# The four sums of a Strassen quarter as four separate pieces, multiplied in the order T1, T2, T3, T4

## The chip, the core and the metric

The kernel runs on one core of a Trainium2 chip. TensorE multiplies matrices, VectorE and ScalarE work elementwise, GpSimd does a handful of tiny operations, and SyncE only issues DMAs. Each engine takes its own list of instructions strictly in order and waits on counting semaphores. The metric is the time of one execution on the device in microseconds (us); three executions of the kernel before took 1846.04, 1846.70 and 1846.81 us.

## The reference

Two layers over 256 tokens of width 2048, all in float32. The part that matters here is the MLP, which both layers have:

```python
def sqrelu_mlp(h, w_in, w_out):
    u = jax.nn.relu(h @ w_in)      # w_in  2048 x 8192
    return (u * u) @ w_out         # w_out 8192 x 2048

for l in range(DEPTH):             # DEPTH = 2
    if l < N_A_LAYERS:
        h = h + multiscale_pool_mixer(rms_norm(h, mix_norm[l]), pool_w[l], pool_scale[l])
    else:
        h = h + diff_attention(rms_norm(h, mix_norm[l]), k, v, w_q[j], lam[j], subln[j], w_o[j], cos, sin, l)
    h = h + sqrelu_mlp(rms_norm(h, mlp_norm[l]), w_mlp_in[l], w_mlp_out[l])
    if l == N_A_LAYERS - 1:
        k, v = shared_kv(h, kv_norm, w_kv, cos, sin)
return rms_norm(h, final_norm)
```

## The kernel before

**High and low halves.** Every weight is loaded as float32 into a raw buffer (`raw` or a part of `arena`; two halves of four pieces each, a piece being 128 x 1024 elements, 512 KB). ScalarE rounds it to `w_hi` (operations `hi_...`), VectorE computes `w_lo = raw - w_hi` (operations `lo_...`), and TensorE takes three matmuls for each product: hi x hi, hi x lo, lo x hi (`product`, L1356 to L1358). `w_hi` and `w_lo` have 8 slots, and a slot holds one piece.

**Pairs.** An MLP is cut into 8 column pairs p = 0 to 7 of 1024 hidden columns. For each p from 1 to 7, TensorE runs `in_pair(p)`, then `out_pair(p - 1)`, then `turn_u(p)`, 16 transposes of the finished hidden values. (In pairs 1 and 7 `turn_u` stands within other work.) Pairs 2 to 5 run in a hardware loop (`Fori`, two pairs in its body, so twice round), where the values waited for are computed in registers; pairs 1, 6 and 7 are written out. With two layers there are 14 such pairs: 8 in loops, 6 written out.

**One `in_pair`.** It has four units: mixed unit 1, a plain unit, mixed units 2 and 3. A mixed unit is one step of Strassen's scheme over a quarter of the weights with raw pieces a, b, c, d. VectorE makes four sums in place: T1 = a + b (in b), T2 = d + T1 (in d), T3 = T2 - a (in a), T4 = c + T2 (in c). TensorE takes seven products of six matmuls each: P1 and P2, P3 on plain pieces, P5 on T1 and P7, P4, P6 on the others. Each goes to a PSUM bank of its own. In unit 1 the banks must first be free of the previous pair's hidden values, so P7, P4 and P6 wait for `u_taken`, which VectorE's `u_low` raises.

**Order on the helpers at the end of unit 3.** VectorE (`mix_lo_lots`): split T1, sum T2, sum T3, sum T4, split T3, then one double-width split of T4 and T2 together (`lo_pair`). ScalarE (`mix_hi_lots`): round T1, round T3 once its sum is there, then round T4 and T2 with one double-width instruction (`hi_sums`). Next come the first steps of `out_pair`. ScalarE: `copy_p1` (L606, saves bank P1), then rounding of the first two double pieces of `w_mlp_out`. VectorE: split of the first double piece, then `c_11` (L951), the sum that empties bank P2. TensorE's first matmul of `out_pair` waits for both that split and `c_11` (`lo_ready`, `c_added`).

**Loads.** SyncE reloads a raw half as soon as `lo_ready` says that its pieces have been split; the counts are in `in_pair` and `out_pair` of the sync block (L403 to L431).

Of the kernel before, what the change touches and what calls it, by code (L numbers as in the profile page):

```python
# [23 lines left out]
F32 = mybir.dt.float32  # L24
F32R = mybir.dt.float32r
ACT = mybir.ActivationFunctionType
ALU = mybir.AluOpType
# [101 lines left out]
def trunk(nc, x, mix_norm, mlp_norm, pool_w, pool_scale, kv_norm, w_kv, w_q, lam, subln, w_o,  # L129
          w_mlp_in, w_mlp_out, final_norm, keep_consts, pool_consts, out):  # L130
    with ExitStack() as ctx:
# [101 lines left out]
        O_BANKS = ((B_P1, B_P2), (B_P3, B_P5))  # L233
        U_BANKS = (B_P7, B_P4, B_P6, B_22)
        END_BANKS = ((B_P1, B_P2), (B_P4, B_22), (B_P1, B_P2), (B_P4, B_22), (B_P3, B_P5), (B_P4, B_22), (B_P3, B_P5), (B_P4, B_22))
# [135 lines left out]
        def _(sp):  # L371
# [35 lines left out]
            def in_pair(layer, p):  # L407
                at = i_at(layer, p)
                if isinstance(p, int) and p == 0:
                    in_unit(layer, 0, 0, 0, at - 2, at)  # L410
                    if layer == 0:
                        sp.wait_ge(x_squared, 1)
                        sp.wait_ge(ssq_done, 3)
                    else:
                        sp.wait_ge(o_done, 2 * PAIRS)
                    in_unit(layer, 0, 1, 1, None, None)
                    in_unit(layer, 0, 2, 0, at + 2, at + 4)
                    in_unit(layer, 0, 3, 1, at + 6, at + 8)
                    return
                in_unit(layer, p, 1, 0, at - 6, at - 4)  # L420
                in_unit(layer, p, 0, 1, at - 2, at)
                in_unit(layer, p, 2, 0, at + 6, at + 8)
                in_unit(layer, p, 3, 1, at + 10, at + 12)

            def out_pair(layer, p):
                at = o_at(layer, p)
                for g in range(NG):
                    free = (at - 10, at - 2, at + 2, at + 6)[g]
                    load_unit(g % 2, [out_view[layer][:, bass.ds(p * 8 + 2 * i, 2), SW * g:SW * (g + 1)] for i in range(4)],
                              free, free + 2)  # L430

# [67 lines left out]
        def _(act):  # L499
# [19 lines left out]

            def hi_sums(at, slot, half, cd, summed):  # L520

                act.wait_ge(w_summed, summed)
                act.wait_ge(pe_done, at - 6)
                nc.scalar.activation(w_hi[:, slot:slot + 2], raw_half[half][:, 2 * cd:2 * cd + 2], ACT.Copy).then_inc(hi_ready, 2)  # L524

            def mix_hi_lots(at, slot, half, landed, sums, lots):

                for lot in lots:
# [7 lines left out]
                    elif lot == 2:  # L536
                        hi_sum(at + 4, spot, half, 1, sums + 1)
                        hi_sum(at + 5, spot + 1, half, 0, sums + 3)
                    else:
                        hi_sums(at + 6, spot, half, 1, sums + 4)  # L540

# [297 lines left out]
        def _(dve):  # L839
# [31 lines left out]

            def mix_lo_lots(at, slot, half, sums, lots):

                a, b, c, d = (raw_half[half][:, i] for i in range(4))
                for lot in lots:
                    spot = (slot + 2 * lot) % HALVES
                    if lot == 0:
                        dve.wait_ge(hi_ready, at + 2)
                        nc.vector.tensor_tensor(w_lo[:, spot], a, w_hi[:, spot].bitcast(F32), ALU.subtract).then_inc(lo_ready, 2)
                    elif lot == 2:  # L880
                        lo_sum(at + 4, spot, half, 1)
                        dve.wait_ge(w_summed, sums + 1)
                        dve.wait_ge(lo_ready, at + 4)
                        nc.vector.tensor_tensor(d, d, b, ALU.add).then_inc(w_summed, 1)  # L884
                        dve.wait_ge(w_summed, sums + 2)
                        nc.vector.tensor_tensor(a, d, a, ALU.subtract).then_inc(w_summed, 1)  # L886
                        nc.vector.tensor_tensor(c, c, d, ALU.add).then_inc(w_summed, 1)  # L887
                        lo_sum(at + 5, spot + 1, half, 0)
                    else:
                        lo_pair(at + 2 * lot, spot, half, lot % 2)  # L890

# [110 lines left out]
            def in_pair(layer, p, par):  # L1002
# [9 lines left out]
                if not second:  # L1012
                    out_add(layer, p - 2, 3)
                mix_lo_lots(at, slot, 0, sums, (3,))
                u_low(layer, p - 1, False)
                for cd in range(2):
                    lo_pair(at + 8 + 2 * cd, slot + 2 * cd, 1, cd)
                t1_sum(0, i_landed(layer, p, 2))
                mix_lo_lots(at + 12, (slot + 4) % HALVES, 0, sums + 4, (0, 1, 2))
                t1_sum(1, i_landed(layer, p, 3))  # L1020
                mix_lo_lots(at + 12, (slot + 4) % HALVES, 0, sums + 4, (3,))
                mix_lo_lots(at + 20, (slot + 4) % HALVES, 1, sums + 8, range(4))

# [292 lines left out]
        def _(pe):  # L1316
# [110 lines left out]
            def mix_unit(layer, p, u, at, slot, begin, end):  # L1427
# [22 lines left out]
                pe.wait_ge(lo_ready, at + 6)  # L1450
                mixed(B_P7, MIX_S3, u, (slot + 5) % HALVES, begin, end).then_inc(pe_done, 1)
                pe.wait_ge(lo_ready, at + 8)
                if begin:
                    pe.wait_ge(u_taken, done - 2)
                mixed(B_P4, MIX_22, u, (slot + 6) % HALVES, begin, end).then_inc(pe_done, 1)
                if begin:
                    pe.wait_ge(u_taken, done - 1)
                mixed(B_P6, MIX_S2, u, (slot + 7) % HALVES, begin, end).then_inc(pe_done, 1)

# [249 lines left out]
```

## Time and profile before

| | before |
|---|---|
| median of 3 runs | 1846.7 us |
| the profiled execution | 1846.67 us, of which 1844.9 us from its first to its last instruction (the span) |
| TensorE busy | 1799.5 us (98%) |
| VectorE busy | 1426.3 us (77%) |
| ScalarE busy | 977.3 us (53%) |
| DMA | 189 GB/s in the mean |
| mean granted TensorE clock | 0.999 |

The profile records one execution. A row of its timeline gives start, duration, engine, source line, operation, what is written and read, the count of merged instructions and, in brackets, how long the engine stood idle before and whom it waited for. ACT is ScalarE, DVE is VectorE, PE is TensorE. Back-to-back matmuls overlap: a 128 x 512 matmul lasts 0.39 us in the records and starts 0.23 us behind the one before.

### The profile page before, as it was taken

Reading aid. Unit: us, or ns where it says so; the run is one execution under the profiler, and the core shown is the slowest. Engines: PE = TensorE matmul, PEld = TensorE weight load, DVE = VectorE, ACT = ScalarE, POOL = GpSimd, SP = SyncE. Lnnn points to the kernel's source line nnn. Section 1 sums busy time; section 2 is a strip of 40 time slices with the busy share of each in tenths; the row PEclk is TensorE's granted clock in tenths of the full one; section 3 lists DMA queues with packets and bytes.
Section 4 is the critical chain, followed back from the end, with each engine's and each line's share of the span. In section 5 each row is a group of like instructions: output and inputs, shape, how many; then the busy total and the mean of one; then the engine's idle time right before and its main releaser. Section 6 shows DMA issues by size and latency. Waiting matters only on the chain.

```text
span 1844.9 us, 22951 instructions
## 1 busy us (share of the span) xinstructions
PE 1799.5 (98%) x8173; PEld 1487.5 (81%) x8173; DVE 1426.3 (77%) x1380; ACT 977.3 (53%) x1021; POOL 9.2 (0%) x15
## 2 busy tenths in 40 slices
PE   6999999999999999999999999999999999999998
PEld 5778787878787878888888888878787878788786
DVE  6787879788888886755557776788888879787876
ACT  6664655564646454643345545654646455554643
POOL 0000000000000000000000000000000000000000
PEclk9999999999999999999999999999999999999999
DMA  9446656565657474566664446365647474646671
GB/s 317 145 159 206 197 193 218 177 206 193 203 165 240 151 243 151 177 194 190 189 195 146 137 156 223 124 223 184 208 164 243 150 237 136 227 161 206 198 256 69
DMA packets 178487, 348.78 MB, mean 189 GB/s; under 512 B 10642, under 2 KB 10852, under 8 KB 178020
## 3 DMA queue, kind: packets, MB, share of 16 engines
q1 hardware_dynamic: 177696, 345.88, 56.7%
q10 hardware_dynamic: 708, 1.81, 0.3%
q8 instruction: 50, 0.82, 0.2%
q14 instruction: 33, 0.27, 0.0%
HBM read 345.55 MB, written 2.10 MB: 188 GB/s over the span
## 4 chain that ended last, share of the span: by engine, by line
PE 82%; DVE 9%; ACT 5%; issue 3%; DMA 1%; POOL 0%; DVEq 0%; SPq 0%; ACTq 0%; POOLq 0%
PE bank L1356 21%; PE bank L1358 20%; PE bank L1357 20%; PE bank L1332 6%; PE bank L1330 6%; PE bank L1331 6%; DVE w_lo L857 3%; ACT w_hi L512 2%; ACT w_hi L524 2%; PE bank L1377 1%; DVE arena L884 1%; PE bank L1348 1%; DVE w_lo L845 1%; DVE arena L886 1%; DVE arena L887 1%
## 5 line engine op out<-in xcount | busy, mean ns | idle before, releaser
L857 DVE TENSOR_TENSOR w_lo<-raw,w_hi 128x2048 fp32r<-128x2048 f32 x128 | 293.0, 2289 | 107.1 <-ACT w_hi L512 68.0
L1356 PE MATMUL bank<-w_hi,u_hi_a 128*128 128x512 f32 x896 | 350.3, 391 | 0.0
L1358 PE MATMUL bank<-w_hi,u_lo_a 128*128 128x512 f32 x896 | 348.8, 389 | 0.0
L1357 PE MATMUL bank<-w_lo,u_hi_a 128*128 128x512 f32 x896 | 348.7, 389 | 0.0
L857 DVE TENSOR_TENSOR w_lo<-arena,w_hi 128x2048 fp32r<-128x2048 f32 x128 | 291.6, 2287 | 54.6 <-ACT w_hi L512 42.5
L1356 PE MATMUL bank<-w_hi,mix_hi 128*128 128x512 f32 x684 | 269.4, 394 | 20.1 <-DVE w_lo L857 18.5
L512 ACT ACTIVATE w_hi<-arena 128x2048 fp32r<-128x2048 f32 x114 | 217.5, 1918 | 103.9 <-PE bank L1358 100.5
L512 ACT ACTIVATE w_hi<-raw 128x2048 fp32r<-128x2048 f32 x100 | 188.2, 1909 | 157.7 <-PE bank L1358 148.7
L1357 PE MATMUL bank<-w_lo,mix_hi 128*128 128x512 f32 x684 | 266.4, 389 | 0.0
L1358 PE MATMUL bank<-w_hi,mix_lo 128*128 128x512 f32 x684 | 266.3, 389 | 0.0
L505 ACT ACTIVATE w_hi<-raw 128x1024 fp32r<-128x1024 f32 x128 | 133.6, 1062 | 150.6 <-PE bank L1332 143.6
L845 DVE TENSOR_TENSOR w_lo<-raw,w_hi 128x1024 fp32r<-128x1024 f32 x128 | 153.2, 1221 | 73.3 <-ACT w_hi L505 72.8
L1356 PEld LDWEIGHTS bank<-w_hi,u_hi_a 128*128 128x128 f32 x896 | 168.1, 188 | 39.1 <-issue 2.8
L1358 PEld LDWEIGHTS bank<-w_hi,u_lo_a 128*128 128x128 f32 x896 | 168.2, 188 | 35.2
L1357 PEld LDWEIGHTS bank<-w_lo,u_hi_a 128*128 128x128 f32 x896 | 168.2, 188 | 34.3
L979 DVE TENSOR_TENSOR h<-bank,h 128x512 f32<-128x512 f32 x168 | 107.9, 684 | 93.0 <-PE bank L1358 75.0
L1356 PEld LDWEIGHTS bank<-w_hi,mix_hi 128*128 128x128 f32 x684 | 128.4, 188 | 52.0 <-DVE w_lo L857 24.4
L1358 PEld LDWEIGHTS bank<-w_hi,mix_lo 128*128 128x128 f32 x684 | 128.4, 188 | 27.0
L1357 PEld LDWEIGHTS bank<-w_lo,mix_hi 128*128 128x128 f32 x684 | 128.5, 188 | 25.7
L1332 PE MATMUL bank<-w_hi,a_lo 128*128 128x512 f32 x352 | 137.1, 390 | 0.0
L518 ACT ACTIVATE w_hi<-raw 128x1024 fp32r<-128x1024 f32 x56 | 59.6, 1064 | 141.8 <-DVE raw L886 120.4
L1330 PE MATMUL bank<-w_hi,a_hi 128*128 128x512 f32 x320 | 126.1, 394 | 0.0
(173 smaller groups left out, 2598.3 us busy)
## 6 DMA issues: line engine op xcount, KB each, us to landing
raw<-in_w_mlp_in SPq DMA_DIRECT2D x128, 512.0 KB, 4.5
arena<-in_w_mlp_in SPq DMA_DIRECT2D x128, 512.0 KB, 5.3
raw<-in_w_mlp_out SPq DMA_DIRECT2D x128, 512.0 KB, 5.0
arena<-in_w_mlp_out SPq DMA_DIRECT2D x128, 512.0 KB, 4.9
raw<-in_w_kv SPq DMA_DIRECT2D x64, 512.0 KB, 4.5
raw<-in_w_q SPq DMA_DIRECT2D x32, 512.0 KB, 4.6
raw<-in_w_o SPq DMA_DIRECT2D x32, 512.0 KB, 4.0
raw<-in_pool_w SPq DMA_DIRECT2D x8, 512.0 KB, 7.5
```

The source lines that it names most:

```text
L505: nc.scalar.activation(w_hi[:, strip_slot(s, n)], raw[:, n % RAW], ACT.Copy).then_inc(hi_ready, 1)
L512: nc.scalar.activation(w_hi[:, slot:slot + 2], raw_half[half][:, 2 * cd:2 * cd + 2], ACT.Copy).then_inc(hi_ready, 2)
L518: nc.scalar.activation(w_hi[:, slot], raw_half[half][:, i], ACT.Copy).then_inc(hi_ready, 1)
L845: nc.vector.tensor_tensor(w_lo[:, slot], raw[:, n % RAW], w_hi[:, slot].bitcast(F32), ALU.subtract).then_inc(lo_ready, 1)
L857: nc.vector.tensor_tensor(w_lo[:, slot:slot + 2], raw_half[half][:, 2 * cd:2 * cd + 2], w_hi[:, slot:slot + 2].bitcast(F32), ALU.subtract) ...
L979: last = nc.vector.tensor_tensor(h[:, tb, cols], banks[tb][:], h[:, tb, cols], ALU.add)
L1330: nc.tensor.matmul(banks[tb][:], hi[:, tok], w_hi[:, n, kk, :], start=begin, stop=False)
L1331: nc.tensor.matmul(banks[tb][:], hi[:, tok], w_lo[:, n, kk, :], start=False, stop=False)
L1332: last = nc.tensor.matmul(banks[tb][:], lo[:, tok], w_hi[:, n, kk, :], start=False, stop=end)
L1356: nc.tensor.matmul(bank[:], hi, w_hi[:, slot, kk, :], start=begin, stop=False)
L1357: nc.tensor.matmul(bank[:], hi, w_lo[:, slot, kk, :], start=False, stop=False)
L1358: return nc.tensor.matmul(bank[:], lo, w_hi[:, slot, kk, :], start=False, stop=end)
```

## The change

The pair {T4, T2} of `hi_sums`/`lo_pair` is taken apart. The four sums now go through the engines as T1, T2, T3, T4: each is rounded by an instruction of its own, split by one of its own, and waited for by itself. On VectorE the split of T2 comes between sum T3 and sum T4. TensorE's products follow: P5 on T1, then P6 on T2, P7 on T3 and P4 on T4. The banks that `turn_u` fills (`U_BANKS`) change their order in the same way. The raw pieces a and b are free when T3 is split and c and d when T4 is, so SyncE's waits move by one count.

```diff
-        U_BANKS = (B_P7, B_P4, B_P6, B_22)
+        U_BANKS = (B_P6, B_P7, B_P4, B_22)
...
-                in_unit(layer, p, 2, 0, at + 6, at + 8)
+                in_unit(layer, p, 2, 0, at + 7, at + 8)
...
-                    free = (at - 10, at - 2, at + 2, at + 6)[g]
+                    free = (at - 9, at - 1, at + 2, at + 6)[g]
...
-                              free, free + 2)
+                              free, (at - 8, at, at + 4, at + 8)[g])
...
                         hi_sum(at + 4, spot, half, 1, sums + 1)
-                        hi_sum(at + 5, spot + 1, half, 0, sums + 3)
+                        hi_sum(at + 5, spot + 1, half, 3, sums + 2)
                     else:
-                        hi_sums(at + 6, spot, half, 1, sums + 4)
+                        hi_sum(at + 6, spot, half, 0, sums + 3)
+                        hi_sum(at + 7, spot + 1, half, 2, sums + 4)
...
+                    elif step == 2:
+                        lo_sum(at + 4, tail, half, 1)
                         dve.wait_ge(w_summed, sums + 1)
                         dve.wait_ge(lo_ready, at + 4)
                         nc.vector.tensor_tensor(d, d, b, ALU.add).then_inc(w_summed, 1)
                         dve.wait_ge(w_summed, sums + 2)
                         nc.vector.tensor_tensor(a, d, a, ALU.subtract).then_inc(w_summed, 1)
+                        lo_sum(at + 5, tail + 1, half, 3)
                         nc.vector.tensor_tensor(c, c, d, ALU.add).then_inc(w_summed, 1)
-                        lo_sum(at + 5, spot + 1, half, 0)
+                    elif step == 3:
+                        lo_sum(at + 6, tail + 2, half, 0)
                     else:
-                        lo_pair(at + 2 * lot, spot, half, lot % 2)
+                        lo_sum(at + 7, tail + 3, half, 2)
...
                 pe.wait_ge(lo_ready, at + 6)
-                mixed(B_P7, MIX_S3, u, (slot + 5) % HALVES, begin, end).then_inc(pe_done, 1)
-                pe.wait_ge(lo_ready, at + 8)
+                mixed(B_P6, MIX_S2, u, (slot + 5) % HALVES, begin, end).then_inc(pe_done, 1)
                 if begin:
                     pe.wait_ge(u_taken, done - 2)
-                mixed(B_P4, MIX_22, u, (slot + 6) % HALVES, begin, end).then_inc(pe_done, 1)
+                pe.wait_ge(lo_ready, at + 7)
+                mixed(B_P7, MIX_S3, u, (slot + 6) % HALVES, begin, end).then_inc(pe_done, 1)
                 if begin:
                     pe.wait_ge(u_taken, done - 1)
-                mixed(B_P6, MIX_S2, u, (slot + 7) % HALVES, begin, end).then_inc(pe_done, 1)
+                pe.wait_ge(lo_ready, at + 8)
+                mixed(B_P4, MIX_22, u, (slot + 7) % HALVES, begin, end).then_inc(pe_done, 1)
```

The order on **VectorE** at the end of unit 3 of pair 1 and the start of `out_pair`, before. The 1024-wide `w_lo` rows are the splits of T1 and T3, the three `arena<-arena` rows the sums T2, T3, T4, the 2048-wide ones the split of {T4, T2} and the first of `out_pair`, and L951 is `c_11`:

```order
77 L863 TENSOR_TENSOR w_lo<-arena,w_hi 128x1024
78 L884 TENSOR_TENSOR arena<-arena 128x1024
79 L886 TENSOR_TENSOR arena<-arena 128x1024
80 L887 TENSOR_TENSOR arena<-arena 128x1024
81 L863 TENSOR_TENSOR w_lo<-arena,w_hi 128x1024
82 L857 TENSOR_TENSOR w_lo<-arena,w_hi 128x2048
83 L857 TENSOR_TENSOR w_lo<-raw,w_hi 128x2048
84 L951 TENSOR_TENSOR arena<-bank,arena 128x512
```

The same place on VectorE in the changed kernel:

```order
78 L858 TENSOR_TENSOR w_lo<-arena,w_hi 128x1024
79 L881 TENSOR_TENSOR arena<-arena 128x1024
80 L883 TENSOR_TENSOR arena<-arena 128x1024
81 L858 TENSOR_TENSOR w_lo<-arena,w_hi 128x1024
82 L885 TENSOR_TENSOR arena<-arena 128x1024
83 L858 TENSOR_TENSOR w_lo<-arena,w_hi 128x1024 x2
84 L852 TENSOR_TENSOR w_lo<-raw,w_hi 128x2048
85 L950 TENSOR_TENSOR arena<-bank,arena 128x512
```

The split of T2 has moved ahead of sum T4, and T3 and T4 follow as two single splits.

The same place on **ScalarE**, before: rounding of the plain pieces c and d, of T1 and T3, of {T4, T2}, then `copy_p1` and the first rounding for `out_pair`:

```order
65 L512 ACTIVATE w_hi<-arena 128x2048
66 L518 ACTIVATE w_hi<-arena 128x1024 x2
67 L524 ACTIVATE w_hi<-arena 128x2048
68 L606 ACTIVATE arena<-bank 128x512
69 L512 ACTIVATE w_hi<-raw 128x2048 x2
```

The same place on ScalarE in the changed kernel:

```order
64 L512 ACTIVATE w_hi<-arena 128x2048
65 L518 ACTIVATE w_hi<-arena 128x1024 x4
66 L601 ACTIVATE arena<-bank 128x512
67 L512 ACTIVATE w_hi<-raw 128x2048 x2
68 L613 ACTIVATE arena<-arena,rms 128x512
```

Four single roundings stand in a row, and `copy_p1` (now L601) is still behind the last of them.

## Rows read from the trace of the kernel before

**Rows 1.** Waits of TensorE: who waited for whom, us in total, times, longest.

```profile
PE bank L1356 <- DVE w_lo L857: 18.5, 14, 1.4
...
PE bank L1643 <- DVE arena L1277: 1.7, 1, 1.7
```

**Rows 2.** Timeline of TensorE, pair 3, end of unit 3 (start us, duration, instruction, idle before).

```profile
305.85 0.39 PE L1356 MATMUL bank<-w_hi,mix_hi 128*128 128x512 f32 x1
...
308.34 0.39 PE L1358 MATMUL bank<-w_hi,mix_lo 128*128 128x512 f32 x1
310.01 0.50 PE L1356 MATMUL bank<-w_hi,mix_hi 128*128 128x512 f32 x1 [1.28 <-DVE w_lo L857]
...
312.97 0.49 PE L1356 MATMUL bank<-w_hi,u_hi_a 128*128 128x512 f32 x1
```

**Rows 3.** Timeline of VectorE over the same stretch of pair 3.

```profile
301.95 1.22 DVE L884 TENSOR_TENSOR arena<-arena 128x1024 f32<-128x1024 f32 x1
303.20 1.23 DVE L886 TENSOR_TENSOR arena<-arena 128x1024 f32<-128x1024 f32 x1
304.35 1.22 DVE L887 TENSOR_TENSOR arena<-arena 128x1024 f32<-128x1024 f32 x1
305.63 1.23 DVE L863 TENSOR_TENSOR w_lo<-arena,w_hi 128x1024 fp32r<-128x1024 f32 x1
307.66 2.29 DVE L857 TENSOR_TENSOR w_lo<-arena,w_hi 128x2048 fp32r<-128x2048 f32 x1 [0.80 <-ACT w_hi L524]
309.94 2.29 DVE L857 TENSOR_TENSOR w_lo<-raw,w_hi 128x2048 fp32r<-128x2048 f32 x1
312.15 0.68 DVE L951 TENSOR_TENSOR arena<-bank,arena 128x512 f32<-128x512 f32 x1
```

**Rows 4.** Timeline of ScalarE over the same stretch of pair 3.

```profile
304.54 1.06 ACT L518 ACTIVATE w_hi<-arena 128x1024 fp32r<-128x1024 f32 x1 [5.09 <-DVE arena L886]
305.64 1.92 ACT L524 ACTIVATE w_hi<-arena 128x2048 fp32r<-128x2048 f32 x1
307.47 0.58 ACT L606 ACTIVATE arena<-bank 128x512 f32<-128x512 f32 x1
307.94 3.71 ACT L512 ACTIVATE w_hi<-raw 128x2048 fp32r<-128x2048 f32 x2
```

**Rows 5.** Timeline of VectorE and ScalarE, pair 1 (written out), the same place.

```profile
128.94 1.22 DVE L884 TENSOR_TENSOR arena<-arena 128x1024 f32<-128x1024 f32 x1
...
131.45 1.06 ACT L518 ACTIVATE w_hi<-arena 128x1024 fp32r<-128x1024 f32 x1 [5.01 <-DVE arena L886]
...
134.46 0.58 ACT L606 ACTIVATE arena<-bank 128x512 f32<-128x512 f32 x1
```

**Rows 6.** Timeline of VectorE and ScalarE, pair 2 of the second layer (loop).

```profile
1304.18 1.21 DVE L884 TENSOR_TENSOR arena<-arena 128x1024 f32<-128x1024 f32 x1
...
1309.78 0.58 ACT L606 ACTIVATE arena<-bank 128x512 f32<-128x512 f32 x1
```

**Rows 7.** Timeline, pair 1, unit 1: VectorE, ScalarE, TensorE; last row VectorE in unit 3.

```profile
101.02 2.29 DVE L857 TENSOR_TENSOR w_lo<-raw,w_hi 128x2048 fp32r<-128x2048 f32 x1 [5.62 <-ACT w_hi L524]
103.23 2.48 DVE L974 TENSOR_TENSOR u_lo_a<-bank,u_hi_a 128x512 fp32r<-128x512 f32 x4
...
101.89 2.06 ACT L626 ACTIVATE u_hi_a<-bank 128x512 fp32r<-128x512 f32 x4 [0.97 <-PE bank L1377]
...
103.96 0.50 PE L1356 MATMUL bank<-w_hi,mix_hi 128*128 128x512 f32 x1 [0.81 <-DVE u_lo_a L974]
...
125.60 2.29 DVE L857 TENSOR_TENSOR w_lo<-arena,w_hi 128x2048 fp32r<-128x2048 f32 x1 [0.42 <-ACT w_hi L512]
```

**Rows 8.** Pair 3: VectorE in unit 1, ScalarE's first rounding of unit 2; loads (page).

```profile
270.29 1.29 DVE L979 TENSOR_TENSOR h<-bank,h 128x512 f32<-128x512 f32 x2 [0.55 <-PE bank L1358]
...
278.01 1.04 ACT L533 ACTIVATE w_hi<-raw 128x1024 fp32r<-128x1024 f32 x1
...
raw<-in_w_mlp_in SPq DMA_DIRECT2D x128, 512.0 KB, 4.5
```

More of the change, by code:

```diff
@@ L518, in hi_sum @@
                 nc.scalar.activation(w_hi[:, slot], raw_half[half][:, i], ACT.Copy).then_inc(hi_ready, 1)
[L520 to L524, printed above, removed]
             def mix_hi_lots(at, slot, half, landed, sums, lots):
@@ L870, in t1_sum, with mix_lo_lots @@
                 nc.vector.tensor_tensor(b, a, b, ALU.add).then_inc(w_summed, 1)
-            def mix_lo_lots(at, slot, half, sums, lots):
+            def mix_lo_lots(at, slot, half, sums, steps):
                 a, b, c, d = (raw_half[half][:, i] for i in range(4))
-                for lot in lots:
-                    spot = (slot + 2 * lot) % HALVES
-                    if lot == 0:
+                tail = (slot + 4) % HALVES
+                for step in steps:
+                    if step == 0:
                         dve.wait_ge(hi_ready, at + 2)
-                        nc.vector.tensor_tensor(w_lo[:, spot], a, w_hi[:, spot].bitcast(F32), ALU.subtract).then_inc(lo_ready, 2)
-                    elif lot == 2:
-                        lo_sum(at + 4, spot, half, 1)
+                        nc.vector.tensor_tensor(w_lo[:, slot], a, w_hi[:, slot].bitcast(F32), ALU.subtract).then_inc(lo_ready, 2)
+                    elif step == 1:
+                        lo_pair(at + 2, (slot + 2) % HALVES, half, 1)
+                    elif step == 2:
+                        lo_sum(at + 4, tail, half, 1)
                         dve.wait_ge(w_summed, sums + 1)
@@ L1013, in in_pair @@
                     out_add(layer, p - 2, 3)
-                mix_lo_lots(at, slot, 0, sums, (3,))
+                mix_lo_lots(at, slot, 0, sums, (3, 4))
                 u_low(layer, p - 1, False)
@@ L1018, in in_pair @@
                 t1_sum(0, i_landed(layer, p, 2))
-                mix_lo_lots(at + 12, (slot + 4) % HALVES, 0, sums + 4, (0, 1, 2))
+                mix_lo_lots(at + 12, (slot + 4) % HALVES, 0, sums + 4, (0, 1, 2, 3))
                 t1_sum(1, i_landed(layer, p, 3))
-                mix_lo_lots(at + 12, (slot + 4) % HALVES, 0, sums + 4, (3,))
-                mix_lo_lots(at + 20, (slot + 4) % HALVES, 1, sums + 8, range(4))
+                mix_lo_lots(at + 12, (slot + 4) % HALVES, 0, sums + 4, (4,))
+                mix_lo_lots(at + 20, (slot + 4) % HALVES, 1, sums + 8, range(5))
             def out_pair(layer, p, par):
```

## The prediction

> **What bounds the kernel now.** I first read who TensorE waits for, since it is busy for 98% of the span. Outside the start of the program the list is nearly one line: 18.5 us in 14 waits on VectorE's split at L857 [rows 1]. Fourteen is the number of pairs, 7 in each layer, so I opened the timeline of one. In unit 3 of pair 3 TensorE runs its products without a gap, 11 matmuls from 305.85 to 308.34, or 0.226 us each and 1.36 us a product. It then stands still until 310.01, and the first matmul of `out_pair` starts at 312.97 [rows 2]. The other engines show why. VectorE splits {T4, T2} from 307.66 to 309.95, and could not start earlier since ScalarE rounded them until 307.56 [rows 3, 4]. The wait costs 310.01 - 308.34 - 0.23 = 1.44 us of start-to-start time.
>
> The rows behind the stall matter more. `out_pair` begins at 312.97, 0.14 us after `c_11` ended at 312.15 + 0.68 = 312.83 [rows 2, 3]. `c_11` stands right behind the split of the first `out_pair` piece (309.94). That split waited for its rounding (307.94 plus half of 3.71, about 309.8), which follows `copy_p1` (307.47), which follows the rounding of {T4, T2} [rows 3, 4]. So **the start of `out_pair` already hangs on ScalarE's chain**: sums, last rounding, `copy_p1`, rounding, split, `c_11`. From `copy_p1` to TensorE it is 312.97 - 307.47 = 5.50 us. TensorE has only 0.1 us of slack against it, and the change leaves these links as they are. I therefore ask two things: does TensorE's own stall go, and does `copy_p1` start earlier or later?
>
> **TensorE's stall goes.** Take pair 3. T2's sum ends at 301.95 + 1.22 = 303.17. ScalarE starts on a loop sum 304.54 - (303.20 + 1.23) = 0.11 us after its end, and VectorE starts a single split 305.63 - (304.54 + 1.06) = 0.03 us after its rounding [rows 3, 4]. So T2 is rounded from 303.28 to 304.34 and its split starts at 304.37, just as VectorE is free of sum T3 (303.20 plus a pitch of 1.15, which is 304.35 - 303.20). T2 is ready at 305.6, and TensorE wants it at 305.85 + 1.36 = 307.21. Sum T4 starts at 305.51 and ends at 306.73. T3, rounded by 305.60 as now, is split from about 306.66 to 307.88, wanted at 308.57. T4 is rounded from 306.84 to 307.90 and split from 307.93 to 309.15, wanted at 309.93. Every piece is early, the last two by 0.7 us. TensorE would finish unit 3 at 309.93 + 1.36 = 311.29, some 1.6 us earlier than now.
>
> **But the gain does not reach `out_pair`.** ScalarE starts its next instruction 0.97 us after a single rounding of 1.06 (it overlaps by 0.09, as 307.47 against 305.64 + 1.92 = 307.56 shows [rows 4]). So `copy_p1` starts at 306.84 + 0.97 = 307.81 and not at 307.47: **0.34 us later**. The reason is the order on VectorE. Sum T4, on which the last rounding waits, now has the split of T2 in front of it (1.14 us), and that is more than the rounding gains by being half as long. The chain behind is the same, so `out_pair` starts at about 313.31. TensorE stands for 313.31 - 311.29 = 2.0 us there: the stall moves from inside unit 3 to the start of `out_pair` and the pair takes 0.34 us more.
>
> In short, from the start of sum T2 to the start of `copy_p1` it is now 307.47 - 301.95 = 5.52 us in the first layer's loop, and becomes 1.22 + 0.11 + 1.06 + 0.03 + 1.14 + 1.22 + 0.11 + 0.97 = 5.86. In the second layer's loop it is now 1309.78 - 1304.18 = 5.60 [rows 6], so the loss is 0.26. In the written-out pairs it is 134.46 - 128.94 = 5.52, but ScalarE starts only 131.45 - (130.19 + 1.23) = 0.03 us behind a sum, where 130.19 is 128.94 plus the 1.25 by which sum T3 follows sum T2 in rows 3 [rows 3, 5]. There T2's rounding is over at 131.25, before VectorE is free at 131.34. Sum T4 starts at 132.48 and ends at 133.70, and `copy_p1` starts at 133.73 + 0.97 = 134.70, 0.24 later. Sum: 4 x 0.34 + 4 x 0.26 + 6 x 0.24 = **+3.84 us**.
>
> **The entry of each MLP gains a little.** In unit 1 of pair 1 TensorE waits 0.81 us for the first `u_low`, which VectorE starts at 103.23, straight behind its double split (101.02), while ScalarE's part of it was ready from 101.89 + 0.58 = 102.47 (a rounding from a bank takes 0.58) [rows 4, 7]. Two single splits hand over earlier. The double rounding ended at 0.10 before 101.02 and took 1.90, so it ran from 99.02. Single ones end at 100.08 and 101.05, and the splits are over by 101.25 + 1.22 = 102.47. `u_low` can start at 102.50, 0.73 earlier. Of this only part lasts. Later in the pair VectorE's split at 125.60 had waited just 0.42 us, plus about 0.08 of overlap, and the changed order puts one more instruction boundary (0.03) before it, so it moves by 0.47 [rows 7]. Twice that is **-0.94 us**.
>
> **What costs nothing.** In units 1 and 2 the pieces are split well ahead of TensorE. The loads of unit 2 go out later: a and b now follow T3's split, which stands behind the addition at 270.29 (1.29 us). That is 271.5 + 1.15 = 272.7, and 4.5 us more gives 277.2, while ScalarE wants the first at 278.01 [rows 8]. The margin is 0.8 us. If it is used up, ScalarE waits inside its own idle time, so I take 0. The other unit 3 loads move by about 1 us against several us of cover. The changed banks cost nothing, since each `u_low` (0.6 us) stays ahead of a product of 1.36 us.
>
> **The sum.** 3.84 - 0.94 = +2.9 us. The profiled execution took 1846.67 us (span 1844.9 and 1.8 around it), which is the median of 1846.7 within 0.03. So 1846.7 + 2.9 = **1849.6 us**. Unknown is the handover to the two new roundings. From below: 0.03 everywhere, as in the written-out pairs, makes the loops 0.24 and 0.16, the sum 3.0 and the time 1848.8. From above: rivals 2 and 3.
>
> **Rival 1: the stall simply goes (faster).** If `out_pair` started when TensorE is done with unit 3, a pair would gain 312.97 - 311.29 = 1.68 us and the 0.1 of a restart, about 1.7 for 14 pairs = 24 us: 1823. For it: the one big line in the waits, and engines with spare time. Against it: `c_11` ends 0.14 before `out_pair`, with ScalarE's chain unbroken before it. The Trainium skill (Perfetto Trace Analysis, Optimizing Scalar/DVE Operations) says that where these engines are not saturated but cause bubbles elsewhere, breaking up instructions may let work complete sooner. By that rule the time is this rival's. The rows agree for the product that waits and disagree for the chain behind it. Chance 0.09.
>
> **Rival 2: each new handover costs more (slower).** The second layer's loop takes 0.08 us longer than the first's for the same instructions, so a wait on a computed value can cost more than 0.11. With 0.08 more on both new handovers everywhere, the pairs lose 0.50, 0.42 and 0.40: 4 x 0.50 + 4 x 0.42 + 6 x 0.40 = 6.1, less 0.94, is +5.1: 1851.8. It decides from 0.06 more per pair on (3.7 us in all). Chance 0.24.
>
> **Rival 3: the entry gain does not come**, since something else is late in pair 1 (a transfer, or the round of ReLUs ahead of T3's rounding). Then +3.8: 1850.5. Chance 0.07.
>
> **Rival 4: sum T4 is not on the chain** after all, and `copy_p1` starts as now. Then only the entry counts: 1845.8. Chance 0.06.
>
> **Rival 5: the clock.** The new gap of about 1.9 us is longer than any mid-program gap so far, of which the longest outside the 14 is 1.7 [rows 1], with a mean granted clock of 0.999. If the gap brought the clock to 1.2 GHz for just one product (six matmuls, 0.23 us more each), each pair would lose 1.4: 1869. Chance 0.02. The Trainium skill (TensorE: Matmul & The Clock Gate, Why this matters for your kernels) warns of idle gaps between bursts of matmuls. The rows show no drop up to 1.7 us.
>
> **How the numbers follow.** The forecast has 0.52. A difference under 0.2% (3.7 us) can't be told from none, so the forecast and rival 4 count as same (0.58), rivals 2, 3 and 5 as slower (0.33), rival 1 as faster (0.09). The range takes in rival 4 with some slack below, and rival 2 with about 1 us above: 1845.0 to 1853.0, which leaves out rivals 1 and 5 and the tails.
>
> **What would show it.** Right: no TensorE wait on a split in unit 3; 14 waits of about 1.9 us before the first matmul on `u_hi_a`, released by the `c_11` sum or the split ahead of it; their sum near 14 x 1.86 = 26 us in place of the 18.5; `copy_p1` 5.8 us after sum T2 starts; loop pairs about 86.9 us apart; pair 1's wait for `u_low` shrunk from 0.8 to about 0.1 us. Wrong: `out_pair` starting within 0.3 us of unit 3's end (rival 1), `copy_p1` under 5.5 or over 6.0 us behind sum T2 (rivals 4, 2), a granted clock under 1 behind a gap (rival 5), or ScalarE waiting for DMAs in unit 2.

## The result and the profile after

The changed kernel takes 1860.15 us (median of 4 runs, 1858.97 to 1861.93), the kernel before 1846.6 on the same chip. The ratio is 1.0075, with a 95% interval of 1.0057 to 1.0092: **slower by 13.5 us**, where +2.9 was forecast and 1853.0 was the upper end.

TensorE's waits in the changed kernel (line waited at, releaser, us in total, times, longest):

```profile
PE bank L1355 <- DVE arena L950: 25.0, 14, 1.9
PE bank L1560 <- DMA arena<-in_subln: 8.6, 1, 8.6
...
PE bank L1643 <- DVE arena L1276: 1.7, 1, 1.7
PE bank L1355 <- DVE w_lo L852: 1.1, 2, 0.6
```

The fourteen stalls of [rows 1] are gone, and fourteen of up to 1.9 us stand ahead of `out_pair`, released by `c_11` at L950. That is the foreseen move. Longer waits explain 25.0 - 18.5 = 6.5 us at most. The rest is in the page's line of busy time:

```profile
PE 1809.0 (97%) x8173; PEld 1497.4 (80%) x8173; DVE 1426.8 (77%) x1422; ACT 989.5 (53%) x1063; POOL 9.2 (0%) x15
```

Before, TensorE was busy for 1799.5 us with the same 8173 matmuls. It does the same work and needs 9.5 us more for it. The timeline of TensorE in pair 3 of the changed kernel, at the place of [rows 2] (start us, duration, instruction, idle before), shows which ones:

```profile
313.66 0.39 PE L1357 MATMUL bank<-w_hi,mix_lo 128*128 128x512 f32 x1
315.84 0.49 PE L1355 MATMUL bank<-w_hi,u_hi_a 128*128 128x512 f32 x1 [1.79 <-DVE arena L950]
316.17 0.41 PE L1356 MATMUL bank<-w_lo,u_hi_a 128*128 128x512 f32 x1
316.41 0.60 PE L1357 MATMUL bank<-w_hi,u_lo_a 128*128 128x512 f32 x1
316.80 0.63 PE L1355 MATMUL bank<-w_hi,u_hi_a 128*128 128x512 f32 x1
...
319.36 0.62 PE L1355 MATMUL bank<-w_hi,u_hi_a 128*128 128x512 f32 x1
319.79 0.43 PE L1356 MATMUL bank<-w_lo,u_hi_a 128*128 128x512 f32 x1
320.05 0.39 PE L1357 MATMUL bank<-w_hi,u_lo_a 128*128 128x512 f32 x1
```

Two matmuls behind the gap run as ever, then eight take 0.60 to 0.63 us instead of 0.39 and start 0.43 apart instead of 0.23. From 316.41 to 320.05 are nine steps, 3.64 us, where nine at 0.227 make 2.04: **1.60 us lost**. The windows of TensorE at L1355, four us long from the start of `out_pair` in several pairs, name the reason (stretch, length, PE and PEld busy with counts, granted clock, DMA share, GB/s):

```profile
227.40:231.40 4.00, 2.08 (x4) 1.18 (x4) 0.57 1.00 353
315.80:319.80 4.00, 2.20 (x4) 1.15 (x4) 0.58 0.95 347
581.00:585.00 4.00, 2.45 (x6) 1.13 (x6) 1.00 0.99 344
1324.40:1328.40 4.00, 2.46 (x6) 1.12 (x6) 1.00 0.98 347
```

The granted clock fell from 2.4 to 1.2 GHz for most of the stretch in the first two of these four, with DMA shares alike. The fourth stands behind a gap of 1.88 us, as long as any, and keeps the clock. Over the program the clock falls in seven pairs of fourteen: all four of the first layer's loop and three of four in the second's. It falls in none of the six written-out pairs, where the gap (TensorE's idle time in one piece ahead of `out_pair`) is 1.71 us and not 1.79 to 1.88.

VectorE and ScalarE in pair 3 of the changed kernel, the places of [rows 3, 4]:

```profile
304.55 1.22 DVE L881 TENSOR_TENSOR arena<-arena 128x1024 f32<-128x1024 f32 x1
305.80 1.22 DVE L883 TENSOR_TENSOR arena<-arena 128x1024 f32<-128x1024 f32 x1
306.97 1.23 DVE L858 TENSOR_TENSOR w_lo<-arena,w_hi 128x1024 fp32r<-128x1024 f32 x1
308.12 1.22 DVE L885 TENSOR_TENSOR arena<-arena 128x1024 f32<-128x1024 f32 x1
309.25 2.44 DVE L858 TENSOR_TENSOR w_lo<-arena,w_hi 128x1024 fp32r<-128x1024 f32 x2
312.82 2.29 DVE L852 TENSOR_TENSOR w_lo<-raw,w_hi 128x2048 fp32r<-128x2048 f32 x1 [1.13 <-ACT w_hi L512]
315.03 0.68 DVE L950 TENSOR_TENSOR arena<-bank,arena 128x512 f32<-128x512 f32 x1
```

```profile
305.88 1.06 ACT L518 ACTIVATE w_hi<-arena 128x1024 fp32r<-128x1024 f32 x1 [3.83 <-DVE arena L881]
307.14 1.06 ACT L518 ACTIVATE w_hi<-arena 128x1024 fp32r<-128x1024 f32 x1 [0.20 <-DVE arena L883]
309.37 1.06 ACT L518 ACTIVATE w_hi<-arena 128x1024 fp32r<-128x1024 f32 x1 [1.17 <-DVE arena L885]
310.33 0.58 ACT L601 ACTIVATE arena<-bank 128x512 f32<-128x512 f32 x1
310.81 3.71 ACT L512 ACTIVATE w_hi<-raw 128x2048 fp32r<-128x2048 f32 x2
```

The chain is the one that was drawn: sum T4 (308.12) stands behind the split of T2 (306.97), ScalarE idles 1.17 us for it, and `copy_p1` starts 310.33 - 304.55 = 5.78 us behind sum T2, where it was 5.52 before. From `copy_p1` to TensorE it is 315.84 - 310.33 = 5.51, as before.

The span of the profiled execution grew by 15.25 us (1844.85 to 1860.1; this execution is the slowest of the four). Pair by pair, from the starts of `out_pair` in both traces:

| Part | us |
|---|---|
| before the first MLP | +0.45 |
| entry of each MLP: gain in unit 1, given back in the same unit | -0.70 + 0.70, twice |
| the chain, 14 steps of 0.23 to 0.28 | +3.58 |
| the clock, 7 steps of 1.58 to 1.63 | +11.2 |

### The profile page after: what moved, and what is told of

Read it like the earlier page. It is cut to its first block, busy times and chain, and to the rows that moved or that the text cites. A ratio compares the mean times of both kernels' runs of the same rounds, so it can differ in the third digit from the quotient of the medians.

```text
span 1860.1 us, 23093 instructions
## 1 busy us (share of the span) xinstructions
PE 1809.0 (97%) x8173; PEld 1497.4 (80%) x8173; DVE 1426.8 (77%) x1422; ACT 989.5 (53%) x1063; POOL 9.2 (0%) x15
## 4 chain that ended last, share of the span: by engine, by line
PE 82%; DVE 7%; ACT 6%; issue 3%; DMA 1%; POOL 0%; ACTq 0%; DVEq 0%; SPq 0%; POOLq 0%
PE bank L1355 21%; PE bank L1357 21%; PE bank L1356 20%; PE bank L1331 6%; PE bank L1329 6%; PE bank L1330 6%; ACT w_hi L512 4%; PE bank L1376 1%; DVE w_lo L852 1%; PE bank L1347 1%; DMA raw<-in_w_mlp_in 1%; DVE w_lo L840 1%; DVE arena L881 1%; DVE arena L885 1%; DVE w_lo L858 1%
## 5 line engine op out<-in xcount | busy, mean ns | idle before, releaser
L1355 PE MATMUL bank<-w_hi,u_hi_a 128*128 128x512 f32 x896 | 354.9, 396 | 25.0 <-DVE arena L950 25.0
L1357 PE MATMUL bank<-w_hi,u_lo_a 128*128 128x512 f32 x896 | 353.2, 394 | 0.0
L1356 PE MATMUL bank<-w_lo,u_hi_a 128*128 128x512 f32 x896 | 353.2, 394 | 0.0
L852 DVE TENSOR_TENSOR w_lo<-arena,w_hi 128x2048 fp32r<-128x2048 f32 x114 | 259.7, 2287 | 64.6 <-ACT w_hi L512 64.3
L852 DVE TENSOR_TENSOR w_lo<-raw,w_hi 128x2048 fp32r<-128x2048 f32 x100 | 228.9, 2289 | 94.8 <-ACT w_hi L512 94.8
L1355 PE MATMUL bank<-w_hi,mix_hi 128*128 128x512 f32 x684 | 267.7, 391 | 0.2
L1355 PEld LDWEIGHTS bank<-w_hi,u_hi_a 128*128 128x128 f32 x896 | 170.9, 191 | 66.4 <-DVE w_lo L852 18.0
L505 ACT ACTIVATE w_hi<-raw 128x1024 fp32r<-128x1024 f32 x128 | 133.6, 1062 | 150.6 <-PE bank L1331 144.2
L840 DVE TENSOR_TENSOR w_lo<-raw,w_hi 128x1024 fp32r<-128x1024 f32 x128 | 153.2, 1221 | 73.4 <-ACT w_hi L505 73.0
L518 ACT ACTIVATE w_hi<-raw 128x1024 fp32r<-128x1024 f32 x112 | 118.8, 1062 | 156.1 <-DVE raw L881 86.8
L1355 PEld LDWEIGHTS bank<-w_hi,mix_hi 128*128 128x128 f32 x684 | 128.4, 188 | 26.7 <-DVE u_lo_a L973 0.7
L858 DVE TENSOR_TENSOR w_lo<-raw,w_hi 128x1024 fp32r<-128x1024 f32 x112 | 135.3, 1218 | 8.5 <-ACT w_hi L518 8.5
```

Source lines behind the costliest of these rows:

```text
L505: nc.scalar.activation(w_hi[:, strip_slot(s, n)], raw[:, n % RAW], ACT.Copy).then_inc(hi_ready, 1)
L518: nc.scalar.activation(w_hi[:, slot], raw_half[half][:, i], ACT.Copy).then_inc(hi_ready, 1)
L840: nc.vector.tensor_tensor(w_lo[:, slot], raw[:, n % RAW], w_hi[:, slot].bitcast(F32), ALU.subtract).then_inc(lo_ready, 1)
L852: nc.vector.tensor_tensor(w_lo[:, slot:slot + 2], raw_half[half][:, 2 * cd:2 * cd + 2], w_hi[:, slot:slot + 2].bitcast(F32), ALU.subtract) ...
L858: nc.vector.tensor_tensor(w_lo[:, slot], raw_half[half][:, i], w_hi[:, slot].bitcast(F32), ALU.subtract).then_inc(lo_ready, 1)
L1355: nc.tensor.matmul(bank[:], hi, w_hi[:, slot, kk, :], start=begin, stop=False)
```

## Experiments

Diffs are against the changed kernel unless another is named. In this table "idle" is TensorE's idle time in one piece ahead of `out_pair`, and "falls" are pairs of 14 in which the granted clock fell behind it, both from the profiled execution.

| Kernel | us | ratio to before (95%) | idle, written out / loops | falls |
|---|---|---|---|---|
| changed | 1860.15 | 1.0057 to 1.0092 | 1.71 / 1.79 to 1.88 | 7 |
| `after_again` | 1859.17 | 1.0042 to 1.008 | 1.71 / 1.79 to 1.89 | 5 |
| `split_gap` | 1850.4 | 1.001 to 1.0029 | 1.32 to 1.38 | 0 |
| `after_copy_twice` | 1876.41 | 1.0142 to 1.0176 | 2.33 / 2.42 to 2.52 | 11 |
| `after_pad` | 1887.39 | 1.0202 to 1.0236 | 1.45 to 1.69 | 0 |
| `before_pad` | 1914.84 | 1.0345 to 1.038 | 1.67 to 1.70 / 1.76 to 1.78 | 5 |
| `old_order_singles` | 1847.74 | 0.9996 to 1.0016 | 1.51 / 1.64 to 1.66 | 0 |
| `copy_early` | 1843.63 | 0.9974 to 0.9993 | 1.23 / 1.31 to 1.41 | 0 |
| `c11_early` | 1835.01 | 0.9916 to 0.9949 | 0.63 to 0.72 | 0 |
| `lot0_singles` | 1821.56 | 0.9845 to 0.9878 | none | 0 |
| `lot0_again` | 1821.51 | 0.9847 to 0.9879 | none | 0 |
| `entry_singles` | 1820.13 | 0.9838 to 0.9871 | none | 0 |
| `before_lot0` | 1844.55 | 0.9979 to 0.9998 | none; 1.3 to 1.5 in unit 3 | 0 |

### Is it the clock, and is it there again?

The changed kernel once more, unedited.

> The changed kernel once more, beside the next three on the same chip. Theory G (one gap): in each of 14 pairs all of TensorE's waiting has moved into one gap of 1.7 to 1.9 us before out_pair, and behind such a gap the granted clock sometimes falls to half; each fall costs 1.6 us (pair intervals of 88.4 instead of 86.8 us). The chain alone costs 14 x 0.26 = 3.6 us, so the time is 1850.3 plus 1.6 for each fall: 1858 to 1862 with 5 to 8 falls, all in the loop pairs, where the gap is 1.79 us or longer, none in the written-out ones (1.71 us). Rival O (order or luck): the falls came from that one chip or execution; then this run shows none and 1850.

Slower again, by 12.6 us in the medians (1859.17 against 1846.56), with single executions from 1854.27 to 1860.11. The pairs that fall differ: there are five. In the first layer's loop they are those at 313.89 and 402.30, while the two at 227.07 and 490.76 have the same gap and keep the clock. Windows of TensorE at L1355, as above:

```profile
227.00:231.00 4.00, 2.44 (x6) 1.12 (x6) 1.00 0.99 366
313.80:317.80 4.00, 2.14 (x4) 1.03 (x4) 0.65 1.03 389
```

So a gap of 1.8 to 1.9 us makes a fall likely (12 of 16 over both kernels' loops) and not certain. What decides between two equal gaps is open. Equal gaps also come at different moments, and no run varied the moment alone.

### Break the gap in two

In unit 3 the last product (P4) also waits for ScalarE's first double rounding for `out_pair`. TensorE then idles a little earlier, and starts `out_pair` no earlier or later than it would have.

```diff
+                if u == 3:
+                    pe.wait_ge(hi_ready, at + 10)
                 pe.wait_ge(lo_ready, at + 8)
```

> The changed kernel, but in unit 3 TensorE's last product (P4) also waits until ScalarE has rounded the first out_pair piece, which is over about 0.2 to 0.3 us after TensorE could start P4. The chain that starts out_pair is untouched. Theory G: the gap of 1.8 us comes apart into about 0.2 and 1.4 us, the clock stays at 1.0 and the time is 1846.7 + 3.6 = 1850 us, 8 to 11 us under the changed kernel. Rival S (what counts is the sum of the idle time near the end of a pair, or the new order of the products): as many falls as in the changed kernel and 1860 us.

Measured 1850.4. TensorE in pair 3:

```profile
310.88 0.49 PE L1355 MATMUL bank<-w_hi,mix_hi 128*128 128x512 f32 x1 [0.15 <-ACT w_hi L512]
...
313.88 0.49 PE L1355 MATMUL bank<-w_hi,u_hi_a 128*128 128x512 f32 x1 [1.35 <-DVE arena L950]
```

An added wait makes the kernel 9.8 us faster. `out_pair` starts where it started (313.88 here, 313.89 in `after_again`), the idle time is in two pieces, and no pair falls. The chain is untouched, so 1850.4 is what the changed kernel costs without the clock: +3.8 us. The recorded idle time adds up to 0.15 + 1.35 = 1.50 us here and not 1.79. Matmuls overlap in the records (0.39 us long, 0.227 apart), so each stop hides 0.16 us of standstill. So this run shows what the falls cost, and leaves open whether the sum near the end of a pair would do as well as one piece. `before_pad` below speaks against the sum.

### A longer gap

`copy_p1` is done twice, the second after the first, with no tensor added. It puts about 0.6 us more into the chain.

```diff
+                nc.scalar.activation(p1_copy, B_P1[:], ACT.Copy).then_inc(p1_first, 1)
+                act.wait_ge(p1_first, p + 7 * layer)
```

> The changed kernel with copy_p1 done twice, the second time behind a wait for the first: about 0.6 us more in ScalarE's chain and no tensor added, so that every tensor lies where it lay. (The pad kernels had 128 bytes more in front of some tensors, and each of their matmuls took 232 instead of 227 ns, which alone is some 30 us; so they didn't lengthen the gap.) The gap before out_pair grows from 1.7 to 2.3 us in the written-out pairs and from 1.8-1.9 to 2.4-2.5 in the loops. Theory G with length as the cause: falls of the clock in written-out pairs too, 10 to 14 in all. Time: 1850.3 + 14 x 0.6 = 1858.7 plus 16 to 22 = 1875 to 1881. Rival L (falls belong to the loops): 5 to 8 falls, 1867 to 1871.

Measured 1876.41, with eleven falls. The gap grew from 1.71 to 2.33 us in the written-out pairs, and four of those six, which never fell before, now do. Windows from three written-out pairs (stretch, length, granted clock, DMA share, GB/s):

```profile
141.40:145.40 4.00, 0.61 0.94 332
675.10:679.10 4.00, 1.00 0.95 328
1687.70:1691.70 4.00, 0.60 1.04 356
```

So falls don't belong to the loops. Behind these longer gaps the clock can be down before TensorE restarts: in the pair at 497.60 the first matmul already takes 0.79 us, where it takes 0.49 elsewhere.

```profile
497.60 0.79 PE L1358 MATMUL bank<-w_hi,u_hi_a 128*128 128x512 f32 x1 [2.42 <-DVE arena L953]
```

### Two attempts that measured something else

Tiny copies on ScalarE were meant to lengthen the chain, in the changed kernel (two) and in the kernel before (twenty, behind its own order). Both write to a new tensor of 128 bytes per partition.

```diff
+        pad = sb("pad", [P, 32])
...
+                for k in range(2):
+                    nc.scalar.activation(pad[:, k:k + 1], keep[:, C_IDENT:C_IDENT + 1], ACT.Copy)
```

> The changed kernel with two tiny ScalarE copies (128 x 1) between copy_p1 and the first out_pair rounding, each worth about 0.1 to 0.2 us, so that the one gap before out_pair grows by 0.2 to 0.4 us: 1.9 to 2.1 in the written-out pairs, 2.0 to 2.3 in the loops. Theory G with length as the cause: falls of the clock now also in written-out pairs (none in 12 at 1.71 us so far) and in more loop pairs (12 of 16 so far), 10 to 14 in all. Time 1850.3 + 14 x 0.3 + 1.6 for each fall = 1871 to 1877. Rival L (falls belong to the loops, whatever the gap): still 5 to 8, only in loops: 1863 to 1867.

> The kernel before with 20 tiny ScalarE copies (128 x 1) at that same place: the order of products, splits and roundings is the old one and the 1.3 us stall in unit 3 stays, but out_pair starts 2 to 4 us late, behind a gap of its own. Theory G: a gap of over 1.8 us there brings falls of the clock with the old order too, 1.6 us each, in 7 or more of 14 pairs: about 1846.6 + 14 x 2.5 = 1882 from the delay, and 11 to 22 more from the clock. Rival O (the falls come from the new order of products): granted clock at 1.0 from start to end and only the delay.

Both expectations failed. In `after_pad` the gap became shorter (1.45 to 1.69 us), nothing fell, and yet the time was 1887.39. `before_pad` took 1914.84 where some 1893 to 1904 was expected, with five falls and not seven or more. The line of busy time of `after_pad` and its costliest group, then the same group of `split_gap`, which has no fall either:

```profile
PE 1837.9 (97%) x8173; PEld 1494.4 (79%) x8173; DVE 1427.9 (76%) x1422; ACT 991.0 (53%) x1091; POOL 9.1 (0%) x15
...
L1358 PE MATMUL bank<-w_hi,u_hi_a 128*128 128x512 f32 x896 | 355.6, 397 | 22.1 <-DVE arena L953 22.1
```

```profile
L1355 PE MATMUL bank<-w_hi,u_hi_a 128*128 128x512 f32 x896 | 350.3, 391 | 18.9 <-DVE arena L950 18.9
```

The matmuls of 512 columns are 6 ns longer (397 against 391 ns), and they start 0.2325 us apart instead of 0.227 (the pitch). That makes 1837.9 us of busy TensorE against 1800.6: 37 us, all over the program. The wider pitch is there from 22 us on, while the first tiny copy starts at 136.8, so it isn't the copies running. What is left is the tensor, which nothing on TensorE reads, but which moves the tensors allocated behind it. A kernel with the tensor and no copies was not run, so this cause is argued. The chip is not the cause: `c11_early` and `lot0_singles` ran on the same one with 0.227. The shorter gap fits this, since a slower TensorE arrives later at a chain that didn't slow down. As tests of the gap's length neither kernel is clean, because two things changed at once.

`before_pad` still answers one question, whether it is the new order itself that loses the clock. TensorE there, in a loop pair, where the twenty copies opened a gap ahead of `out_pair` too:

```profile
319.99 0.50 PE L1359 MATMUL bank<-w_hi,mix_hi 128*128 128x512 f32 x1 [0.98 <-DVE w_lo L860]
...
324.81 0.50 PE L1359 MATMUL bank<-w_hi,u_hi_a 128*128 128x512 f32 x1 [1.77 <-DVE arena L954]
```

and its windows at L1359, behind that gap and in a written-out pair:

```profile
324.80:328.80 4.00, 2.34 (x4) 1.03 (x4) 0.59 0.86 265
143.10:147.10 4.00, 2.48 (x6) 1.13 (x6) 1.00 0.85 279
```

The old order, with a gap of 1.77, falls as well (5 of its 8 loop pairs at 1.76 to 1.78, none of six at 1.67 to 1.70). So the new order isn't needed for a fall, and a gap is enough. In the six pairs without a fall a stall of 0.95 to 1.00 us stands some 4.8 us ahead of the gap, over 2.6 us of idle time in sum. That sum alone doesn't do it. Since these gaps have such a stall before them and another pitch, they don't belong in one count with the others.

### Which part of the edit costs the 0.26 us?

The kernel before, with {T4, T2} rounded and split as two singles but the order T1, T3, T4, T2 kept (diff against before, ScalarE's part):

```diff
-                        hi_sums(at + 6, spot, half, 1, sums + 4)
+                        hi_sum(at + 6, spot, half, 2, sums + 4)
+                        hi_sum(at + 7, spot + 1, half, 3, sums + 4)
```

> The kernel before with the double instruction of {T4, T2} cut into two single ones, T4 first, then T2, and TensorE waiting for each; the order T1, T3, T4, T2 and of the sums is kept. If the loss in the chain comes from T2's split standing ahead of sum T4 (1.14 us), here it is only what two single roundings take more than a double one (2 x 0.97 - 1.83 = 0.11 us, plus up to 0.03): out_pair 0.14 us later than before, TensorE's stall in unit 3 gone, one gap of 1.55 to 1.65 us before out_pair. 14 x 0.14 = +2: 1848.6 us without falls of the clock, which by theory G should be rare at this gap. If instead cutting the pair is what costs, out_pair is 0.26 later as in the changed kernel, the gap is 1.8 and the time 1858 or more.

Measured 1847.74, not told apart from before. ScalarE in pair 3, where sum T2 starts at 302.50:

```profile
305.09 3.15 ACT L518 ACTIVATE w_hi<-arena 128x1024 fp32r<-128x1024 f32 x3 [5.08 <-DVE arena L887]
308.14 0.57 ACT L607 ACTIVATE arena<-bank 128x512 f32<-128x512 f32 x1
```

`copy_p1` starts 5.64 behind sum T2, against 5.52 before and 5.78 with the change. Singles alone cost 0.12, and the new order 0.14, in which sum T4 stands behind T2's split. The idle time is in one piece here too, but 1.66 at most, and it doesn't fall.

### Shorten the chain

Three repairs, one on top of the other. First, `copy_p1` goes between the roundings of T2 and T3, where ScalarE idles in the changed order:

```diff
+                        if after_t2 is not None:
+                            after_t2()
...
-                copy_p1(layer, p + 1)
```

> The changed kernel with ScalarE's copy_p1 moved ahead of T3's rounding in unit 3, where ScalarE is idle. Theory C (ScalarE's chain of last rounding, copy_p1, first out_pair rounding starts out_pair): the first out_pair rounding starts 0.47 us earlier, so each pair gains 0.47 on the changed kernel: out_pair 0.2 us earlier than before the change, gap about 1.3 us. With theory G no fall of the clock is left: 1846.7 + 3.6 - 14 x 0.47 = 1843.7 us. Rival D (VectorE's own work sets the start of out_pair): the start does not move, falls stay, 1860 us.

Measured 1843.63. ScalarE in pair 3:

```profile
303.10 1.06 ACT L518 ACTIVATE w_hi<-arena 128x1024 fp32r<-128x1024 f32 x1 [3.83 <-DVE arena L882]
304.07 0.58 ACT L603 ACTIVATE arena<-bank 128x512 f32<-128x512 f32 x1
304.54 1.05 ACT L518 ACTIVATE w_hi<-arena 128x1024 fp32r<-128x1024 f32 x1
306.59 1.06 ACT L518 ACTIVATE w_hi<-arena 128x1024 fp32r<-128x1024 f32 x1 [1.00 <-DVE arena L886]
307.56 1.90 ACT L512 ACTIVATE w_hi<-raw 128x2048 fp32r<-128x2048 f32 x1
```

The rounding for `out_pair` now starts 0.97 behind T4's, with no copy between. Before the repair the two were 310.81 - 309.37 = 1.44 us apart, so the chain is 0.47 us shorter in each pair.

Second, VectorE does `c_11` ahead of the split of the first `out_pair` piece:

```diff
+                c_11(layer, p + 1)
                 out_lots(layer, p, 4 * par + LATER * layer, (0,))
-                c_11(layer, p + 1)
```

> The changed kernel with copy_p1 early, as in the run before, and VectorE's sum c_11 ahead of the split of the first out_pair piece, where VectorE waits for ScalarE anyway. out_pair now waits for that split alone and starts about 0.65 us earlier than with copy_p1 early: gap 0.7 us. 1843.6 - 14 x 0.65 = 1834.5 us, no fall of the clock. If VectorE had no such idle time there, the gain would be under 0.2 us a pair: 1841 or more.

Measured 1835.01. TensorE now waits for the split (L853) and not for `c_11`, 0.63 to 0.72 us (two of the sixteen waits are the entry's, see below):

```profile
PE bank L1356 <- DVE w_lo L853: 10.9, 16, 0.7
```

Third, the first `out_pair` piece is rounded and split as two singles, and TensorE waits for the first alone:

```diff
+                    if lot == 0:
+                        lo_sum(at, slot % HALVES, 0, 0)
+                        lo_sum(at + 1, slot % HALVES + 1, 0, 1)
+                        continue
...
+                        if g == 0 and i < 2:
+                            pe.wait_ge(lo_ready, at + i + 1)
```

> As c11_early, and the first double piece of out_pair rounded and split as two single ones, TensorE waiting for the first one alone. By the chain the first split is over 1.1 us earlier, before TensorE ends unit 3, so no gap is left in a pair: about 1.7 us a pair under the kernel before, 1846.6 - 14 x 1.7 = 1823 us, which is what the change would have given had the stall simply gone. If another wait comes up (c_11, the next pieces), a gap of 0.3 us or more stays and the time is 1827 to 1834.

Measured 1821.56. TensorE passes from unit 3 to `out_pair` without standing still:

```profile
306.89 0.39 PE L1368 MATMUL bank<-w_hi,mix_lo 128*128 128x512 f32 x1
307.12 0.39 PE L1366 MATMUL bank<-w_hi,u_hi_a 128*128 128x512 f32 x1
```

The same kernel once more, beside the two that follow:

> The same kernel as lot0_singles, as the measure for the next one on the same chip: 1821.6 us; TensorE's only waits inside the pairs are two of 0.57 us (pair 1 of each layer, first plain piece of w_mlp_in).

Measured 1821.51.

### What is the change itself worth?

The three repairs in the kernel before, without the change (`copy_p1` goes behind T1's rounding there).

> The kernel before, without the change, with the three repairs of the chain behind it (copy_p1 early, c_11 ahead, the first out_pair piece as two single ones). If the change's own worth is TensorE's stall in unit 3, that stall of 1.3 us stays here and only the small gap before out_pair goes (0.1 us and 0.1 of a restart a pair): 1846.7 - 14 x 0.2 = 1844 us, 22 us over lot0_singles, all of which the change then brings once the chain behind it is short. If the repairs alone did the work: 1825 to 1830 and a smaller stall.

Measured 1844.55. The stall of [rows 1] stays where it was:

```profile
PE bank L1367 <- DVE w_lo L864: 18.7, 14, 1.5
```

So the repairs alone bring 1.9 us (against 1846.43 on that chip), the change alone costs 13.5, and both together bring 25. With the chain short, the change is worth 1844.55 - 1821.51 = 23.0 us, or 1.65 us a pair, which is what rival 1 had computed (1.7).

### The entry of the MLP

`lot0_singles` with the first plain double piece of pair 1's unit 1 as two singles (VectorE's part, diff against `lot0_singles`):

```diff
+                    if cd == 0 and second:
+                        lo_sum(at + 8, slot, 1, 0)
+                        lo_sum(at + 9, slot + 1, 1, 1)
+                        continue
```

> lot0_singles with the first plain double piece of pair 1 also rounded and split as two single ones, and TensorE waiting for the first alone. In the changed kernel the 0.7 us that the earlier u_low gave in unit 1 of pair 1 were lost again five us later at this piece. If its double rounding and split are the cause, the two waits of 0.57 us and their restarts go: 2 x 0.7 = 1.4 us less, 1820.2 us. If the raw load or TensorE's slots were the cause, the waits stay and the time is the same.

Measured 1820.13, and the two waits of 0.57 us (one in each layer) are gone. In the changed kernel they look so in pair 1, first TensorE, then VectorE and ScalarE:

```profile
103.71 0.50 PE L1355 MATMUL bank<-w_hi,mix_hi 128*128 128x512 f32 x1
...
108.65 0.50 PE L1355 MATMUL bank<-w_hi,std_hi 128*128 128x512 f32 x1 [0.57 <-DVE w_lo L852]
```

```profile
106.30 4.49 DVE L852 TENSOR_TENSOR w_lo<-arena,w_hi 128x2048 fp32r<-128x2048 f32 x2 [0.86 <-ACT w_hi L512]
...
104.26 3.75 ACT L512 ACTIVATE w_hi<-arena 128x2048 fp32r<-128x2048 f32 x2
```

This is the fastest version measured, 1.45% under the kernel before.

## Why the prediction was wrong

**TensorE's stall goes: right.** No wait on a split is left in unit 3, and fourteen waits stand ahead of `out_pair`, 25.0 us in sum where 26 was forecast. The links came within a few hundredths: behind sum T2's start, T2's split at 2.42 us (forecast 304.37 - 301.95 = 2.42) and sum T4 at 3.57 (forecast 3.56).

**The chain: right, a little too dear.** Forecast +3.84 us, measured +3.58. The written-out pairs (0.24) and the second layer's loop (0.26) came as computed. The first layer's loop lost 0.27 and not 0.34: T4's rounding starts 309.37 - (308.12 + 1.22) = 0.03 us behind its sum, where I took the 0.11 that the first rounding shows. Rival 2, dearer handovers, is refuted.

**The entry: -0.94 forecast, 0 measured.** This is rival 3 (0.07). Its first half held. `u_low` starts 0.72 earlier and TensorE 103.71 - 0.45 (this trace's later start) = 103.26 against 103.96 in [rows 7]. Five microseconds on it is given back: at 108.65 TensorE waits 0.57 us for the split of the plain double piece, whose rounding (104.26) stands behind ScalarE's round of `u_high`, which the change doesn't move. In the kernel before, TensorE reached this place at 108.20 just as the split was over, with no wait recorded. I asked who is late next at `out_pair` and not here. The jump from 0.73 to 0.47 rested on a VectorE row in unit 3, behind the place where the gain had gone. `entry_singles` removes the second wait, and gains 1.4 us.

**The clock: the step that failed.** Terms, chain and entry as measured give 1846.7 + 3.6 = 1850.3, and `split_gap`, which is the changed kernel without falls, took 1850.4. That is the 1850.5 of rival 3. The rest of the time is rival 5, to which I gave 0.02. I wrote that the rows show no drop up to 1.7 us, which was true, and took the 0.1 to 0.2 us beyond for safe as well. It was an extrapolation past the longest gap seen outside the start of the program (1.73 us), and the eight gaps in the loops lie beyond it. Its price was near: 1.4 us a pair if one product of six matmuls runs at 1.2 GHz, measured 1.6 with eight. That it was near is in part luck, since no row gave the six. What I mis-sized beside the chance was the count: seven pairs (five when run again), not all fourteen, so 1860 and not 1869. The Trainium skill (TensorE: Matmul & The Clock Gate, Why this matters for your kernels) warns of idle gaps between bursts. It means longer ones than these; here the runs decide, and gaps of 1.79 us were enough.

**Rival 1: wrong here, and right one step on.** The stall didn't simply go, since the chain starts `out_pair`. The rule that breaking up instructions may let work complete sooner (the Trainium skill, Perfetto Trace Analysis, Optimizing Scalar/DVE Operations) gave a loss in this kernel and 23.0 us with the chain repaired (`lot0_singles` against `before_lot0`). Rival 4, sum T4 off the chain, is refuted by the rows: ScalarE idled 1.17 us for that sum, and `copy_p1` started 5.78 us behind sum T2 and not at the old 5.52. `copy_early` adds that the rest of the chain counts too: moving `copy_p1` alone off it brought 6.8 us against `split_gap`.

What stays open: what decides whether a gap of 1.8 to 2.5 us brings a fall. Falls by gap, where it is the only stall near and matmuls start 0.227 us apart: none of 56 from 1.2 to 1.66 us (`before`, `before_lot0`, `old_order_singles`, `copy_early`), none of 12 at 1.71, 12 of 16 at 1.79 to 1.89, 4 of 6 at 2.33, 7 of 8 at 2.42 to 2.52. The one gap of 1.72 to 1.73 us ahead of L1643 in the kernel before, which its eleven variants with that pitch have too, brought no fall in any of the twelve.

## What to carry to other kernels

Before pricing a removed stall, find who starts the next stage: if another engine's chain does, the stall moves there, and it pays only once that chain is shortened too. When a change joins short waits of TensorE into one longer than any that the trace shows, count the clock in with a real chance, and compare with a version in which the same idle time is in two pieces. To lengthen a chain for a test, repeat an instruction that is there, and don't allocate a tensor.

## What the runs showed of the hardware

- The granted clock fell behind 12 of 16 single idle gaps of 1.79 to 1.89 us in a program that is otherwise busy 97% of the time. Such a fall took hold after the restart (two matmuls at full speed in pair 3), lasted about eight matmuls of 512 columns, and cost 1.6 us. Behind a gap of 2.42 us it could take hold before the restart (497.60 in `after_copy_twice`).
- In both kernels with 128 bytes per partition of added allocation, and in no other, 512-column matmuls start 0.2325 us apart instead of 0.227 (397 ns each instead of 391 in `after_pad`): 37 us over the program, more than everything else in this study. The allocation by itself, and which tensor's place does it, was not tried.
- In one loop pair the roundings of T2, T3 and T4 start 0.11, 0.12 and 0.03 us behind the ends of their sums. So the loop alone doesn't set the dearer handover; what does is open.
